# Four edits to a two-block decoder kernel: residues on GpSimd, order of two steps, and an even projection's banks

## What is computed

```python
def _rwkv7_mixer(p, mu, w0, w2, a0, a2, g2, k_k, k_a, r_k, ln_w, ln_b): ...
    # token shift, low-rank gates, kk normed by head, delta rule over 256 steps, layer norm, gate
def _stick_breaking_mixer(p, q_norm, k_norm): ...
    # q, k normed by head; z = q k^T; ls = log_sigmoid(-z); cum = ls @ rev_incl; exp(z + cum + acc) @ v
def _retention_mixer(p, gn_w): ...
def _conformer_conv_mixer(p, dw, db, ln_w, ln_b): ...
    # GLU, causal depthwise convolution of width 31 on 256 channels, layer norm, swish
```

## Time and profile before

| | |
|---|---|
| median of 3 runs | 1906.4 us (1901.58 to 1915.32) |
| the profiled execution | 1906.56 us, its span 1904.6 us |
| busy: TensorE, its weight loads | 97%, 91% of the span |
| busy: VectorE, ScalarE, GpSimd | 70%, 48%, 3% |
| mean granted clock of TensorE | 0.986 of full speed |

### The profile page before, as it was taken

How to read it: one execution, slowest core, us unless ns; L and a number is a source line. 1 busy time by engine, 2 the same in 40 slices (tenths; PEclk the granted TensorE clock), 3 DMA queues, 4 the chain that set the end, 5 groups by cost and what they waited for, 6 DMA issues and landing times.

```text
span 1904.6 us, 35006 instructions
## 1 busy us (share of the span) xinstructions
PE 1845.3 (97%) x14961; PEld 1732.7 (91%) x14961; DVE 1331.2 (70%) x1900; ACT 917.4 (48%) x1072; POOL 63.4 (3%) x32
## 2 busy tenths in 40 slices
PE   9899999999998999999999999999999999989999
PEld 9889999999997999999999888888899988889988
DVE  7975566755589656667465768888879578566675
ACT  5353345434443533444344556777666444444453
POOL 0000000000000000000101010101210000000000
PEclk9899999999998999999999999999999999999999
DMA  8221246555542223544545578898955323334330
GB/s 314 90 90 57 89 166 221 177 177 182 194 139 89 73 76 120 199 169 165 196 156 194 197 242 301 324 335 331 334 215 183 127 89 99 114 100 165 118 126 24
DMA packets 52826, 321.89 MB, mean 169 GB/s; under 512 B 6336, under 2 KB 9664, under 8 KB 20032
## 3 DMA queue, kind: packets, MB, share of 16 engines
q1 hardware_dynamic: 52240, 317.76, 47.8%
q10 hardware_dynamic: 432, 1.90, 0.3%
HBM read 317.01 MB, written 1.05 MB: 167 GB/s over the span
## 4 chain that ended last, share of the span: by engine, by line
PE 78%; DVE 14%; ACT 4%; issue 3%; DMA 0%; POOL 0%; SPq 0%; DVEq 0%; ACTq 0%; POOLq 0%
PE b L393 77%; DVE s_arena L409 5%; DVE s_ring_lo L516 4%; ACT s_wh L418 2%; PE b L2553 1%; DVE s_arena L1442 1%; PE b L2089 0%; DVE s_arena L652 0%; DVE s_arena L412 0%; DVE s_arena L2588 0%; DVE s_roots L409 0%; ACT s_arena L418 0%; DMA s_ring<-experts 0%; POOL s_ring_lo L516 0%; DVE s_Hl L409 0%
## 5 line engine op out<-in xcount | busy, mean ns | idle before, releaser
L516 DVE TENSOR_TENSOR s_ring_lo<-s_ring,s_wh 128x2048 fp32r<-128x2048 f32 (+3 forms) x316 | 661.7, 2099 | 301.8 <-ACT s_wh L418 300.4
L418 ACT ACTIVATE s_wh<-s_ring 128x2048 fp32r<-128x2048 f32 (+3 forms) x332 | 574.2, 1732 | 273.8 <-PE b L393 265.7
L393 PE MATMUL b<-s_Hh,s_wh 128*128 128x256 f32 x2184 | 637.6, 292 | 10.8 <-DVE s_arena_r L3118 4.5
L393 PE MATMUL b<-s_Hl,s_wh 128*128 128x256 f32 x2184 | 620.0, 284 | 0.0
L393 PE MATMUL b<-s_Hh,s_ring_lo 128*128 128x256 f32 x2184 | 619.9, 284 | 0.0
L393 PEld LDWEIGHTS b<-s_Hh,s_wh 128*128 128x128 f32 x2184 | 420.9, 193 | 21.1 <-issue 9.1
L393 PEld LDWEIGHTS b<-s_Hl,s_wh 128*128 128x128 f32 x2184 | 421.2, 193 | 1.1
L393 PEld LDWEIGHTS b<-s_Hh,s_ring_lo 128*128 128x128 f32 x2184 | 420.7, 193 | 0.0
L393 PE MATMUL b<-s_arena_r,s_wh 128*128 128x256 f32 x1536 | 277.0, 281 | 6.6 <-DVE s_arena L409 1.7
L393 PEld LDWEIGHTS b<-s_arena_r,s_wh 128*128 128x128 f32 x1536 | 235.6, 188 | 9.4 <-DVE s_arena L409 2.1
L393 PE MATMUL b<-s_arena_r,s_ring_lo 128*128 128x256 f32 x768 | 215.4, 280 | 0.0
(11 more groups left out here) (198 smaller groups left out, 1776.5 us busy)
## 6 DMA issues: line engine op xcount, KB each, us to landing
s_ring<-fixed SPq DMA_DIRECT2D x158, 1024.0 KB, 4.9
s_ring<-experts SPq DMA_DIRECT2D x95, 1024.0 KB, 5.0
s_ring<-experts SPq DMA_DIRECT2D x48, 768.0 KB, 4.4
s_ring<-fixed SPq DMA_DIRECT2D x24, 256.0 KB, 4.3
s_c<-c SPq DMA_DIRECT2D x1, 1664.0 KB, 17.7
s_ring<-fixed SPq DMA_DIRECT2D x3, 512.0 KB, 5.8
s_arena<-s_arena SPq DMA_DIRECT2D x48, 32.0 KB, 3.2
s_c<-c ACTq DMA_DIRECT2D x1, 1344.0 KB, 5.6
```

The source lines that it names most:

```text
L393: return e.matmul(out, l, r, start=start, stop=True, skip_group_check=True)
L418: return e.activation(out, x, ACT.Copy, scale=scale)
L516: e.tensor_tensor(l_, r_, h_.bitcast(F), SUB).then_inc(*up(engine, z % "lo", i))
```

## The change

- The residues of eight pieces per mixer (MIX_POOL: the three of sb, the four of g3 and b3) go to GpSimd, in that order, behind everything else that it does in a mixer.
- The identity copies go from VectorE to GpSimd, which makes them after "all shifted" and before the residues. The level-0 mask goes from GpSimd to VectorE.
- In nine steps of the plan S stands before C, on all engines.
- Even layer: the attention projections begin in bank 5 instead of 4, TensorE waits before the plan for pieces 5 to 7 only and before the third projection for ez 3, two attention cases wait for other value pieces, and the rounding and residue of exbc 5 are issued one step earlier.

```diff
-        pool_pieces = {li["xd", (p, half, 2)] for p in range(8) for half in range(2)}
+        MIX_POOL = [("sb", 0), ("sb", 1), ("sb", 2), ("g3", 0), ("g3", 1), ("g3", 2), ("g3", 3), ("b3", 0)]
+        pool_pieces = {li[f"{name}{l}", j] for l in range(2) for name, j in MIX_POOL} | {li["xd", (p, half, 2)] for p in range(8) for half in range(2)}
...
-                e.wait_ge(*(on("Y", l, lv - 1) if lv else on("eye", l)))
+                e.wait_ge(*(on("Y", l, lv - 1) if lv else on("eye", l, 64)))
...
-                if q < 2:
-                    eye = ident[HALVES[q], HALVES[q]].unsqueeze(1).broadcast_to([64, 8, 64])
-                    e.tensor_copy(Ym8[HALVES[q]], eye).then_inc(*up("V"))
-                    e.tensor_copy(Xm[HALVES[q]], eye).then_inc(*(up("V", "eye", l) if q else up("V")))
+                if q == 3:
+                    e.wait_ge(*now("V"))
+                    msk = c("lvl")[:, 0:64].unsqueeze(1).broadcast_to([128, 8, 64])
+                    e.tensor_tensor(Am, m3(Gm)[:, :, 0:64], msk, MUL).then_inc(*up("V", "level mask", l, 0))
...
         def rwkv_pool(e, l):
-            msk = c("lvl")[:, 0:64].unsqueeze(1).broadcast_to([128, 8, 64])
-            e.wait_ge(*on("Gm", l, 7))
-            pool_free(e)
-            e.tensor_tensor(Am, m3(Gm)[:, :, 0:64], msk, MUL).then_inc(*up("G", "level mask", l, 0))
+            e.wait_ge(*on("all shifted", l))
+            for rows in HALVES:
+                eye = ident[rows, rows].unsqueeze(1).broadcast_to([64, 8, 64])
+                pool_free(e)
+                e.tensor_copy(Ym8[rows], eye).then_inc(*up("G"))
+                pool_free(e)
+                e.tensor_copy(Xm[rows], eye).then_inc(*up("G", "eye", l, rows.start))
...
-        PLAN = (". .K .K .K" + " .KC" * 4 + " .KCS" * 9 + " .KS" * 5 + " .KC" * 9 + " .K" * 8 + " ." * 13).replace(" ", "")
+        PLAN = (". .K .K .K" + " .KC" * 4 + " .KSC" * 9 + " .KS" * 5 + " .KC" * 9 + " .K" * 8 + " ." * 13).replace(" ", "")
...
             conf_pool(e, l)
             rwkv_pool(e, l)
+            for name, j in MIX_POOL:
+                rest_piece(e, li[f"{name}{l}", j], "G")
...
-                after.append(("out", li["ev", 2 * u], 2 - u))
+                after.append(("out", li["ev", 6 - 2 * u], 1))
...
-            return B[6] if u >= LATE else B[4 + u % 3]
+            return B[6] if u >= LATE else (B[5], B[6], B[4])[u % 3]
...
+                elif u == 2:
+                    e.wait_ge(*on("out", li["ez", 3]))
...
-            for u in range(5, 13):
+            for u in range(5, 8):
                 e.wait_ge(*on("out", li[CONV[u]]))
...
             rounds(e, li["exbc", 2])
+            rounds(e, li["exbc", 3])
...
-                    if 1 <= u <= 10:
+                    if 2 <= u <= 10:
                         rounds(e, li[CONV[u + 2]])
...
+            rests(e, li["exbc", 3])
...
-                if 1 <= u <= 10:
+                if 2 <= u <= 10:
                     rests(e, li[CONV[u + 2]])
```

## The result

The changed kernel takes 1943.15 us in the median of 4 runs (1941.9 to 1944.5), the kernel before 1905.53 (1901.58 to 1915.32) beside it: 1.0191 times as long by the comparison of the runs, with a 95% interval from 1.0173 to 1.0209. It is slower, by about 2%; the forecast was 1930. The runs of the kernel before that stand beside the experiments have medians of 1906.7 to 1907.3, and a distance to the kernel before that an experiment gives is taken from those beside it. The profiled execution took 1941.9 us with a span of 1939.9, 35.3 us longer than the span before.

A forecast was written before the change was run, and what follows sets the result against it. VectorE was taken to bound the mixers' tight stretches, with TensorE busy for 97% of the span overall. 1906.6 + 32 (+16 per mixer) - 8.6 (even layer) = 1930; its own range 1916 to 1948, the whole range 1880 to 1948.

The forecast's parts named there:

- likeliest mechanism: Mixers: GpSimd and VectorE instructions with SBUF inputs (two on VectorE) run one after the other; chance 0.60.
- six residues: removed, hold, covered, low clock: Before the first level product: 13.2 us off VectorE, 27.6 held, 2 covered, 1 for TensorE's low clock.
- identity copies: Four per mixer: 1.3 us off VectorE, which is held for 4 x 0.6 = 2.4 us by the GpSimd copies.
- level mask: Mixers: adds 0.6 us on VectorE; the saved GpSimd hop, covered by matmuls, counted nothing, 1 us at most.
- step order by itself: Mixers: stick step first gives results up to 2.4 us earlier, but VectorE waits for ScalarE: 1 us gained.
- seventh and eighth residue: Mixers: seventh falls before the level product once all is late, 0 to 4.6, taken as 2; last two meet slack.
- even layer, once: Even layer: 4.5 us standing and 2.7 low clock gone, 1.4 of a residue wait: -8.6 us together.
- Held by the six residues: 6 x 4.6: VectorE's chain to the first level product is held 4.6 us by each of six GpSimd residues, 27.6 per mixer.
- Three residues one behind the other: Mixer's beginning, about 52 to 66: GpSimd runs three residues in a row, VectorE getting one contending instruction between each.
- the last two residues meet a VectorE with slack: Mixers, last two of eight residues: VectorE has slack by 130 to 160, busy 18.0 us of 30.
- 20 us instead of 9 in each mixer's first 60 us: Profile sign if right: TensorE idle that long, first wait of many us for the kk sums near 54.
- Rival A: Mixers: hold short or rare, VectorE's chain loses 14 us, TensorE becomes the bound: 1875; chance 0.22 with C, a late GpSimd queue.

The follow-up runs named there:

- E1: Changed kernel with each of the eight GpSimd residues per mixer replaced by three memsets to zero, which read no SBUF: 1895.39 us (0.9939).
- E12: Kernel before with the even layer's part, level mask on VectorE and only the three stick-breaking residues per mixer on GpSimd: 1908.49 us (1.0013).
- E11: Kernel before with only the even layer's part and the level mask on VectorE: 1895.50 us (0.9944).
- E5: Changed kernel with the four identity copies per mixer back on VectorE: 1939.54 us (1.0172).
- E2: Changed kernel with all eight residues per mixer back on VectorE, identity copies staying on GpSimd: 1901.38 us (0.9968).
- E10: Kernel before with the even layer's part, level mask on VectorE and new step order; residues and copies stay on VectorE: 1899.95 us (0.9967).
- E4: Kernel before with the even layer's part alone: 1899.34 us (0.9958).
- E8: Changed kernel with only the last two residues per mixer on GpSimd, the first six back on VectorE: 1913.06 us (1.0037).
- E7: Changed kernel with the last two of the eight residues per mixer back on VectorE: 1928.62 us (1.0114).
- E3: Kernel before with the eight residues per mixer on GpSimd and the level mask on VectorE; old step order, copies and even layer: 1930.69 us (1.0128).
- E6: Changed kernel with the old step order, convolution step ahead of stick step: 1926.65 us (1.0110).
- E9: Changed kernel with the old step order and the last two residues per mixer back on VectorE: 1926.86 us (1.0108).

## Why the prediction was right, and where it was not

The forecast of 1930 was 13 us too low, its range of 1880 to 1948 held the time near its upper end, and its likeliest mechanism is the one that E1 showed. The error would have been larger by 5 us if the mask had not gone the other way than forecast. The sum held against the runs, per mixer:

| term | forecast | measured | from |
|---|---|---|---|
| six residues: removed, hold, covered, low clock | -13.2 + 27.6 - 2 + 1 = +13.4 | +13.8 | half of 13.0 (E12 - E11) and 14.5 (next three, below) |
| identity copies | +2.4 - 1.3 = +1.1 | +1.8 | changed kernel - E5; E2 - E10 gives 0.7 |
| level mask | +0.6 | -1.9 | E11 - E4 |
| step order by itself | -1 | +2.2 | E10 - E11 |
| seventh and eighth residue | +2 and 0 | +6.0 | (16.5 - 4.4) / 2; E8 alone gives 5.8, E7 7.3 |
| even layer, once | -8.6 | -7.7 | E4 |

The next three residues are a remainder: E3 less 7.7 for the even layer less E12 = 1930.7 - 7.7 - 1908.5 = 14.5 for both mixers, the last two being free in the old order. Measured terms give 2 x 21.9 - 7.7 = +36; the changed kernel is 37.6 above the kernel before, or 36 above the medians of it that stand beside the experiments. Several terms are differences of a few us between runs whose intervals overlap, so I estimate that a row can be off by about 1 us.

- The hold. "Held by the six residues: 6 x 4.6" was right in kind: GpSimd's 4.56 us, one held instruction for each. In size it is 22.6 us in the changed kernel's first mixer and 24.2 in E6's, since the fourth residue costs little in the one and part of its hold is covered in the other. So 3 to 5 us were covered where 2 was taken, and if the term still comes out right, the rest of it (by the forecast, TensorE's low clock) must have cost more than the 1 us given to it. No run takes that rest apart: the sum of the term is measured, its parts are not. Held instructions are also not only those with two SBUF inputs: one-input TENSOR_SCALAR is held too. The bound of 3 to 4.6 for the longest tap was a little low, 4.78.
- "Three residues one behind the other": two came so. The third waited 4.24 us for ScalarE's rounding and began at 64.35, though before the change its rounded half was there by 57.9.
- A copy on GpSimd takes 0.82 us and not 0.6.
- The mask. "I count nothing, 1 us per mixer at most", with 0.6 on VectorE's chain, had the wrong sign. The size fits if the hop's 1.59 us and the tap held for 1.05 were both on the path: 2.64, less 0.6 to 0.7 for the product on VectorE, is 2.0 against 1.9 measured. That is argued; no run took the two apart, and the traces put 2.9 of the gain into the first mixer and 0.5 into the second.
- **The step that failed** is "the last two residues meet a VectorE with slack", priced at 0 for the last and at 2 for a seventh that was to fall before the level product. The seventh fell behind it (the first level product runs at 118.6, the seventh residue begins at 121.65), and the two cost 5.8 to 7.3 us per mixer. The sentence was read from the busy share of 130 to 160 in the trace of before, 18.0 of 30 us, which is the slack of the old order. The change itself moves the taps into that place: the last six taps before the convolution's mean now run when the eighth residue does, and TensorE waits 5.3 us for them. E6 and E9 show that the sentence is true of the old order and E7 and E8 that it is false of the new one. The two edits were priced one at a time, each against the trace of before, and their product was left out.
- The step order's own price also has the other sign, +2.2 in place of -1. E11 and E10 give it 4.4 us for both mixers, E9 and E7 only 1.8, where six residues are on GpSimd. The wait for ScalarE, named in the forecast, is not covered any more, since no tap stands ahead of it; that this makes the price is argued.
- TensorE idle for "20 us instead of 9 in each mixer's first 60 us" came out as 17.7 from 43 to 106, with the first long wait at the kk sums, as forecast.
- The even layer came nearly as worked out, 7.7 of 8.6: the standing of 4.5 us and the low clock behind it are gone, and in E4 TensorE's waits for residues from 1425 to 1540 fall from 2.1 to 0.7 us.

Rival A, in which nothing is held, was priced at 1875. E1 comes nearest to it and stands at 1895, but it still holds one-input instructions and keeps the new order, so the price without any hold stays open. No version with a mixer's residues on GpSimd was found that beats the kernel before: E12, with three per mixer the fastest of them, stands level with it (1.0013). Those below it by more than the noise (E2, E4, E10, E11) keep all of them on VectorE and have the new even layer; only the last two on GpSimd in the old order, without the first six, was not run.

## What to carry to other kernels

Before work goes from VectorE to GpSimd, count what both read from SBUF: here a GpSimd residue of 4.56 us mostly cost VectorE 3.4 to 4.6 us once, however small the instruction that met it, so the offload lost where VectorE's saving per piece (2.2 us) was below that. Where VectorE stood or read PSUM the two last residues cost nothing (E6 and E9, 0.2 us), and gained nothing either. Price edits of one change against the schedule that the other edits leave, not against the trace of before: here the new order cost 16.5 us beside the eight residues on GpSimd and 4.4 without them. A short hop over an idle engine is worth pricing like an offload, by its duration and by what it holds; here taking one out gave 3.8 us, with overlapping intervals.

## What the runs showed of the hardware

- A 128x16 product on VectorE (L428) took 4.40 us under a GpSimd residue in the changed kernel and 0.17 us without one in E6.
- A 128x2048 residue on GpSimd that began among 24 taps took 11.62 us and held none of them (changed kernel); in E7 two residues at the same place took 4.96 and 4.59 us and the 24 taps 18.22 instead of 9.59.
- A GpSimd memset of 128x2048 took 1.8 us, held TENSOR_SCALAR 128x256 on VectorE for up to 1.7 us (2060 ns against 408), and left all 70 instructions of the tap's form and the 128x512 product at 53.42 (0.69 us) alone. A GpSimd residue, which reads, held both kinds.
- While GpSimd copies 64x512 tiles, VectorE's scan (L1392, 128x256) takes 1004 ns in the mean, where before it took 678, and the two copies in the middle take 0.90 and 0.89 us where the other two take 0.74 and 0.69. Whether the scan is slowed or held for a third of a us each time, no run took apart.
